# A four-layer decoder trunk: norms, output projections and router logits by token tiles

## The reference

```
for i in range(4):
    y = mixer[i % 3](h)                     # ends in a projection @ w_out to 1024 columns
    h = layer_norm(ALPHA * h + y, ln_mix_g[i], ln_mix_b[i])
    m = grouped_moe(h, w_router, ...)       # scores = sigmoid(h @ w_router); best group, top 2
    h = layer_norm(ALPHA * h + m, ln_ffn_g[i], ln_ffn_b[i])
```

## Time and profile before

| | us |
|---|---|
| Runs of the kernel | 2247.17 median of 3 (2244.17 to 2249.45) |
| The profiled execution | 2245.62, its span 2243.7 |
| TensorE matmul busy | 1977.2 (88% of the span) |
| VectorE busy | 760.4 (34%) |
| ScalarE busy | 492.8 (22%) |
| GpSimd busy | 158.8 (7%) |
| Mean granted TensorE clock | 0.928 of 2.4 GHz |
| Read from device memory | 501.80 MB, 224 GB/s over the span |

### The profile page before, as it was taken

One profiled execution on the slowest core, in us unless ns is written; L12 is line 12 of the kernel. 1 busy time (PEld: TensorE's weight loads), 2 busy tenths in 40 slices (PEclk: granted clock), 3 DMA queues, 4 the chain that ended last, 5 costly groups with the idle time before them and its releaser, 6 DMA issues.

```text
span 2243.7 us, 26143 instructions
## 1 busy us (share of the span) xinstructions
PE 1977.2 (88%) x9378; PEld 1137.2 (51%) x9379; DVE 760.4 (34%) x1564; ACT 492.8 (22%) x941; POOL 158.8 (7%) x96
## 2 busy tenths in 40 slices
PE   6989878999896768889989987899989989679997
PEld 5858744444573443443444534434468678334443
DVE  2435533332304343123322113233344265433324
ACT  2453311222203111012211101112223533111121
POOL 1010020000200030000020003000020000020000
PEclk8999988999996779889999997899989999879999
DMA  9430015999942139338994324679964400249994
GB/s 308 148 115 1 20 75 237 424 427 424 335 166 75 38 121 386 150 131 364 425 337 165 139 107 165 271 327 428 424 245 150 150 1 20 75 164 394 424 424 203
DMA packets 79872, 504.05 MB, mean 225 GB/s; under 512 B 7155, under 2 KB 11300, under 8 KB 54956
## 3 DMA queue, kind: packets, MB, share of 16 engines
q1 hardware_dynamic: 69536, 487.60, 53.9%
q0 software_dynamic: 2304, 8.39, 1.0%
q10 hardware_dynamic: 7948, 6.89, 1.0%
HBM read 501.80 MB, written 1.06 MB: 224 GB/s over the span
## 4 chain that ended last, share of the span: by engine, by line
PE 85%; DVE 10%; issue 3%; ACT 2%; ACTq 1%; DVEq 0%; DMA 0%
PE bank L1662 22%; PE bank L1680 11%; PE bank L1394 10%; PE bank L1400 9%; PE bank L1653 7%; PE bank L1778 5%; PE bank L1420 4%; PE bank L1627 2%; PE bank L1492 1%; PE bank L1483 1%; PE bank L1673 1%; PE bank L1385 1%; PE bank L1497 1%; PE bank L1726 1%; PE bank L1636 1%
## 5 line engine op out<-in xcount | busy, mean ns | idle before, releaser
L1662 PE MATMUL bank<-ring,work 128*64 128x512 f32 x2176 | 489.7, 609 | 15.5 <-DVE work L1231 9.5
L1662 PEld LDWEIGHTS bank<-ring,work 128*64 128x64 f32 x2176 | 156.7, 140 | 339.5 <-issue 332.6
L1680 PE MATMUL bank<-ring,work 128*64 128x512 f32 x1088 | 243.1, 596 | 8.6 <-ACT work L814 4.6
L1394 PE MATMUL bank<-HT,ring 128*128 128x256 f32 x1024 | 229.5, 384 | 0.9 <-DVE HT L865 0.9
L1394 PEld LDWEIGHTS bank<-HT,ring 128*128 128x128 f32 x1024 | 197.6, 193 | 37.3 <-issue 10.7
L1400 PE MATMUL bank<-ring,HT 128*128 128x512 f32 x448 | 195.0, 597 | 1.0 <-DVE HT L865 1.0
L1258 DVE TENSOR_TENSOR work<-bank,work 64x512 f32<-64x512 f32 x64 | 68.2, 1066 | 366.7 <-ACT work L792 366.7
L1653 PE MATMUL bank<-work 128*128 128x128 f32 x1152 | 157.1, 293 | 11.6 <-DVE work L1236 6.7
L1653 PEld LDWEIGHTS bank<-work 128*128 128x128 f32 x1152 | 143.4, 203 | 40.9 <-issue 31.6
L792 ACT ACTIVATE work<-bank 64x512 f32<-64x512 f32 x64 | 37.7, 589 | 526.7 <-PE bank L1662 526.7
L1226 DVE TENSOR_TENSOR work<-bank,lncols 128x512 f32<-128x512 f32 x72 | 49.8, 692 | 302.6 <-PE bank L1653 302.6
(11 more groups left out here) (284 smaller groups left out, 1996.5 us busy)
## 6 DMA issues: line engine op xcount, KB each, us to landing
ring<-in_e_w SPq DMA_DIRECT2D x192, 2048.0 KB, 13.2
ring<-in_a_w_in SPq DMA_DIRECT2D x16, 2048.0 KB, 14.9
ring<-in_c_w_in SPq DMA_DIRECT2D x8, 2048.0 KB, 14.5
ring<-in_b_w_in SPq DMA_DIRECT2D x6, 2048.0 KB, 17.1
ring<-in_a_w_out SPq DMA_DIRECT2D x4, 2048.0 KB, 7.8
ring<-in_c_w_out SPq DMA_DIRECT2D x4, 2048.0 KB, 7.8
ring<-in_b_w_out SPq DMA_DIRECT2D x2, 2048.0 KB, 9.3
gB<-in_ln_mix_g POOLq DMA_DIRECT2D x4, 512.0 KB, 4.1
```

The costliest lines, as they stand in the source:

```text
L1394: ins = mm(dst[:, 0:SEQ], wt[:, k, n * P:(n + 1) * P], HT[:, k, :], start=k == 0, stop=k == KC - 1)
L1662: ins = mm(bank[b][lo:lo + CAP, :], x[:, k, :], wt[:, k, :], start=k == 0, stop=k == KC - 1, skip_group_check=True)
L1680: ins = mm(bank[b][nh * CAP:(nh + 1) * CAP, :], h[:, m, :], w2[:, m, nh * 512:(nh + 1) * 512], start=m == 0, stop=m == 3, skip_group_check ...
```

## The change

- `plan()` gives phases one turn for each chunk and tile, tile 0's eight before tile 1's, on banks 0 to 3 (`k % 4`). `half` places a chunk with `k` below 4 in the lower 256 columns of the bank, the others in the upper. The router's turn goes to bank 4.
- The output projections run tile by tile: both halves of tile 0 and then of tile 1. All their weight units are awaited ahead of the first.
- The norm goes by tiles on VectorE: add, statistics, `rstd`, L908 and the four odd copies of tile 0, then the same for tile 1. ScalarE's root and copies go in the same order. At the experts' end and in the last phase it is the same, and in the gMLP's own norm `rstd` goes by tiles.
- TensorE at a mixer's end: transposes of tile 0, router logits of tile 0, then both for tile 1. At the experts' end: transposes of tile 0, then of tile 1, each behind its own `xhat_ready`.
- GpSimd's and ScalarE's waits on transposes go by the last tile's turn.

The core of the diff:

```diff
@@ -96,8 +96,12 @@
             unit(w_out[:, nh * 512:(nh + 1) * 512].rearrange("(k p) n -> p k n", p=P), ("y", i, TT - 1, nh))
-    for k in range(KC):
-        turns.take(k, "ht", 0, k)
+    def chunks(phase):
+        for tt in range(TT):
+            for k in range(KC):
+                turns.take(k % 4, "ht", phase, k, tt)
+
+    chunks(0)
     turns.take(0, "cols")
...
@@ -398,6 +400,10 @@
             eng.wait_ge(drained[b], n + 1)
+        def half(k, tt):
+
+            return slice(k // 4 * SEQ + tt * P, k // 4 * SEQ + (tt + 1) * P)
+
         def emptied(ins, *key):
...
@@ -584,15 +590,15 @@
             act.dma_start(rel33[0:REL_BUCKETS, :], w["rel_bias"]).then_inc(params_in, 16)
-            def ht_chunks(phase):
+            def ht_chunks(phase, tt):
                 for k in range(0, KC, 2):
-                    ps = wait_data(act, "ht", phase, k)
+                    ps = wait_data(act, "ht", phase, k, tt)[:, half(k, tt)]
+                    dst = HT[:, k, tt * P:(tt + 1) * P]
                     if phase == 0:
-                        emptied(a(HT[:, k, :], ps[:, 0:SEQ], ACT.Copy), "ht", phase, k)
+                        emptied(a(dst, ps, ACT.Copy), "ht", phase, k, tt)
                     else:
                         c = (0 if phase % 2 else 2) * 32 + (phase - 1) // 2 * 8 + k
-                        emptied(a(HT[:, k, :], ps[:, 0:SEQ], ACT.Identity, scale=lncols[:, c:c + 1],
-                                  bias=lncols[:, c + 32:c + 33]), "ht", phase, k)
+                        emptied(a(dst, ps, ACT.Identity, scale=lncols[:, c:c + 1], bias=lncols[:, c + 32:c + 33]), "ht", phase, k, tt)
             ln_count = 0
...
@@ -602,13 +608,14 @@
             rsq = 0
-            def ln_rstd():
+            def ln_rstd(tt):
                 nonlocal rsq
                 rsq += 1
-                ahead(ACT.Sqrt)
+                if not tt:
+                    ahead(ACT.Sqrt)
                 act.wait_ge(var_ready, rsq)
-                a(rs[:, 0, :], mv[:, :, 1], ACT.Sqrt, bias=epsc[:, 0:1]).then_inc(rstd_ready, 1)
+                a(rs[:, 0, tt:tt + 1], mv[:, tt, 1:2], ACT.Sqrt, bias=epsc[:, 0:1]).then_inc(rstd_ready, 1)
             def heads_norm(nn):
...
@@ -840,14 +849,17 @@
                     gmlp(i, j)
-                ln_rstd()
-                if 2 * i + 1 != last_phase:
-                    ht_chunks(2 * i + 1)
+                for tt in range(TT):
+                    ln_rstd(tt)
+                    if 2 * i + 1 != last_phase:
+                        ht_chunks(2 * i + 1, tt)
                 if with_moe:
                     experts(i)
-                    ln_rstd()
-                if i < n_layers - 1:
-                    ht_chunks(2 * i + 2)
+                for tt in range(TT):
+                    if with_moe:
+                        ln_rstd(tt)
+                    if i < n_layers - 1:
+                        ht_chunks(2 * i + 2, tt)
         @block.vector
...
@@ -855,69 +867,59 @@
-            def ht_chunks(phase):
+            def ht_chunks(phase, tt):
                 for k in range(1, KC, 2):
-                    ps = wait_data(dve, "ht", phase, k)
+                    ps = wait_data(dve, "ht", phase, k, tt)[:, half(k, tt)]
+                    dst = HT[:, k, tt * P:(tt + 1) * P]
                     if phase == 0:
-                        emptied(v.tensor_copy(HT[:, k, :], ps[:, 0:SEQ]), "ht", phase, k)
+                        emptied(v.tensor_copy(dst, ps), "ht", phase, k, tt)
                     else:
                         c = (0 if phase % 2 else 2) * 32 + (phase - 1) // 2 * 8 + k
-                        emptied(v.tensor_scalar(HT[:, k, :], ps[:, 0:SEQ], lncols[:, c:c + 1], lncols[:, c + 32:c + 33],
-                                                ALU.mult, ALU.add), "ht", phase, k)
+                        emptied(v.tensor_scalar(dst, ps, lncols[:, c:c + 1], lncols[:, c + 32:c + 33], ALU.mult, ALU.add), "ht", phase, k, tt)
...
-            def rstd(blocks):
+            def rstd(blocks, tt):
                 nonlocal rsq
                 own.wait()
-                for tt in range(TT):
-                    ins = v.bn_aggr(mv[:, tt, :], stats[:, tt, 0:6 * blocks])
-                    if tt < TT - 1:
-                        own.then(ins)
                 rsq += 1
-                ins.then_inc(var_ready, 1)
+                v.bn_aggr(mv[:, tt, :], stats[:, tt, 0:6 * blocks]).then_inc(var_ready, 1)
                 dve.wait_ge(rstd_ready, rsq)
-                own.link(v.reciprocal(rs[:, 0, :], rs[:, 0, :]))
...
+                r = [rs[:, n, tt:tt + 1] for n in range(4)]
+                own.link(v.reciprocal(r[0], r[0]))
...
+            def layer_norm(phase, tt):
+                rstd(2, tt)
...
-                for tt in range(TT):
-                    dst, src = H[:, tt, :], H[:, tt, :]
-                    if phase % 2:
-                        dst, src = XH[:, tt, :].rearrange("t (k p) -> t k p", k=KC), src.rearrange("t (p k) -> t k p", k=KC)
-                    v.tensor_scalar(dst, src, mv[:, tt, 0:1], rs[:, 3, tt:tt + 1],
-                                    ALU.subtract, ALU.mult).then_inc(xhat_ready, 1)
-
-            def add_mixed(i):
+                dst, src = H[:, tt, :], H[:, tt, :]
+                if phase % 2:
+                    dst, src = XH[:, tt, :].rearrange("t (k p) -> t k p", k=KC), src.rearrange("t (p k) -> t k p", k=KC)
+                v.tensor_scalar(dst, src, mv[:, tt, 0:1], rs[:, 3, tt:tt + 1], ALU.subtract, ALU.mult).then_inc(xhat_ready, 1)
+
+            def add_mixed(i, tt):
                 for nh in range(2):
-                    for tt in range(TT):
-                        ps = wait_data(dve, "y", i, tt, nh)
-                        sl = H[:, tt, nh * 512:(nh + 1) * 512]
-                        emptied(v.tensor_tensor(sl, ps[:, :], sl, ALU.add), "y", i, tt, nh)
-                    for tt in range(TT):
-                        wait_copy(dve, "y", i, tt, nh)
-                        block_stats(H, tt, nh)
+                    ps = wait_data(dve, "y", i, tt, nh)
+                    sl = H[:, tt, nh * 512:(nh + 1) * 512]
+                    emptied(v.tensor_tensor(sl, ps[:, :], sl, ALU.add), "y", i, tt, nh)
+                for nh in range(2):
+                    wait_copy(dve, "y", i, tt, nh)
+                    block_stats(H, tt, nh)
...
@@ -1300,9 +1302,13 @@
                         v.tensor_tensor(part(b), bank[b][:, :], part(b), ALU.add).then_inc(drained[b], 1)
-                for b in range(4, 8):
-                    dve.wait_ge(drained[b], first[b] + E // 2)
-                    block_stats(H, (b - 4) // 2, (b - 4) % 2)
+                for tt in range(TT):
+                    for nh in range(2):
+                        dve.wait_ge(drained[4 + 2 * tt + nh], first[4 + 2 * tt + nh] + E // 2)
+                        block_stats(H, tt, nh)
+                    layer_norm(2 * i + 2, tt)
+                    if i < n_layers - 1:
+                        ht_chunks(2 * i + 2, tt)
             steps_done = dve.alloc_register("steps_done_dve")
...
@@ -1377,16 +1380,16 @@
                 return ring[s]
-            def ht_chunks(phase):
+            def ht_chunks(phase, tt):
                 src = XH if phase % 2 else H
                 for k in range(KC):
-                    ps = fill("ht", phase, k)
-                    for tt in range(TT):
-                        ins = tr(ps[:, tt * P:(tt + 1) * P], src[:, tt, k * P:(k + 1) * P], ident)
-                    done(ins, "ht", phase, k)
-                if phase % 2 == 0:
+                    ps = fill("ht", phase, k, tt)
+                    done(tr(ps[:, half(k, tt)], src[:, tt, k * P:(k + 1) * P], ident), "ht", phase, k, tt)
+
+            def ht_in(phase):
+                for tt in range(TT):
                     for k in range(KC):
-                        wait_copy(pe, "ht", phase, k)
+                        wait_copy(pe, "ht", phase, k, tt)
             def rows(dst, wt, n):
...
@@ -1412,12 +1415,12 @@
                     wait_copy(pe, "oT", i, g)
-                for nh in range(2):
-                    wt = next_unit()
-                    for tt in range(TT):
+                wts = [next_unit(), next_unit()]
+                for tt in range(TT):
+                    for nh in range(2):
                         ps = fill("y", i, tt, nh)
                         for h in range(HEADS):
-                            ins = mm(ps[:, :], XT[:, h, tt * P:(tt + 1) * P], wt[:, h, :], start=h == 0, stop=h == HEADS - 1)
+                            ins = mm(ps[:, :], XT[:, h, tt * P:(tt + 1) * P], wts[nh][:, h, :], start=h == 0, stop=h == HEADS - 1)
                         done(ins, "y", i, tt, nh)
...
@@ -1619,20 +1622,23 @@
                     wait_copy(pe, "uT", i, g)
-                for nh in range(2):
-                    pss = [fill("y", i, tt, nh) for tt in range(TT)]
-                    wts = [next_unit(), next_unit()]
-                    for tt in range(TT):
```

(49 more changed lines are left out.)

54 lines of the change are left out of this document (21 added, 33 removed).

## The result

The changed kernel takes 2258.61 us (median of 8 runs, 2253.36 to 2260.77), the kernel before 2245.90 beside it (8 runs). The ratio is 1.0056, 95% interval 1.0042 to 1.0070: 12.7 us slower. Forecast were 20.3 slower, 2266, in a range from 2254 to 2275.

What follows compares the result with a forecast made beforehand. TensorE was 85% of the chain, so time could come only from its waits. Mixers 6.0, experts' ends 9.3, clock 1.0, output 1.6 and start 2.4 sum to 20.3 on 2245.6: forecast 2266 us, range 2254 to 2275.

Steps and rivals of the forecast that it cites:

- the experts' ends: Behind the experts, three places: 13.2 us instead of 10.1 to the next layer's first matmul; +9.3, bounds +2.4 and +4.2 each.
- the output: At the output: the norm chain of 1.6 us runs twice; +1.6, bounds +1.2 and +1.8.
- the start: At the start: with four banks, tile 0's transposes wait for ScalarE's first copy; +2.4, bounds +1.8 and +3.0.
- the clock at layer 1: Layer 1's first matmuls may begin at the low clock after two bursts of transposes; +1.0, for this end alone.
- The mixers' term: Behind four mixers: copies delay tile 1, GpSimd and gather (T+29.5; T: last projection's end); +6.0, bounds +3.2 and +9.6.
- gMLP, ring and residual at nothing: gMLP's norm by tiles, later-freed weights and output units awaited ahead, and GpSimd's residual 1.65 us later: all costed at nothing.
- Rival A: Behind the mixers: routing not tied to GpSimd's start, gather at T+27.5, -2.2 instead of +6.0; 2257.7 us; chance 0.14.
- Rival B: Behind the mixers: GpSimd holds none of the routing, gather at T+23.8, -17.0; 2243 or 2239 us; chance 0.06.

Runs made afterwards that it cites:

- the 2220 us kernel: Kernel before with only mixers by token tiles, GpSimd's residual begun after the first gather's shift, ScalarE alone copying tile 0 behind the mixers: 2220.03 us, ratio 0.9874.

## Why the prediction was right, and where its terms were off

The direction was right, and so was its main cause, the second chain of small steps at the experts' ends, the output and the start: these were forecast at 14.3 with the clock at layer 1, and cost 14 to 15 when made alone. The mixers' term had the right mechanism and the wrong result. It was forecast at +6.0, its gathers came 2.15 later, and taken alone the mixers' order made the kernel 5 to 6 us faster (2.3 against the changed code with everything put back). That the total still fell near the forecast rests on the other terms. The sizes, with the profile's 14.8 for the forecast's 20.3:

- **Mixers, +6.0 forecast, +2.15 measured** (by the gathers). The mechanism held: four copies ahead of tile 1's add, GpSimd later, the gather tied to it. Three sizes were off. VectorE is free at T+1.8, not 2.3, since the copies of the earlier trace rows at half width take 0.38 and bank releases 0.2. GpSimd starts at T+7.2 and not T+7.75. And the gather follows it by 21.4, not 21.8: from the end of the second addition it is 11.0 instead of 11.4. The bound of +3.2 was still too high. (The prediction's own 0.5+4x0.41 is 2.1 and not 2.0; its 2.3 stands between the bounds all the same.)
- **Experts' ends, +9.3 forecast, +7.9 measured.** 12.9 for 13.2, since the transposes with their bank waits took 2.1 us and not 2.3 (0.8 in all); and the forecast took before's 10.1 from layer 0 for all three, while layers 1 and 2 had 10.44 and 10.29 (0.5). The bounds of +2.4 and +4.2 do not come out of the terms named: without the two bank waits and with copies of 0.27 it is +2.2, with 0.5 for each wait and 0.54 for the copy +3.8.
- **The clock at layer 1's start, +1.0 forecast, +2.9 between these two profiles** (that layer's first 80 matmuls 20.43 against 17.50 us), and 0.5 at each of the two later starts. This was the term with the worst reading: I let the clock be low for 3 us of matmuls, and it was low for 5.9, and through both bursts of transposes before them. By the rule that the Trainium skill gives (TensorE: Matmul & The Clock Gate, "Part 1: The HAM clock gate") only sustained activity releases the high clock; the trace agrees, 0.50 until 611. But most of the 2.9 is the state in which before was caught. With both tiles together at the experts' end these 80 matmuls took 17.50 in three profiles and 19.4 to 19.9 in eight; with the ends by tiles 20.43, 19.82 and 20.20, some 0.5 more than the eight. Layer 2's start goes the other way: 36.2 in before and one more profile, 34.6 in nine, 36.4 to 36.7 with the ends by tiles. The rest of layer 1's 4.6 is the clock as well: in after it was low until 768.3, over the first 3.2 us of the output projection, which costs 1.5; in before it had risen just ahead of it.
- **Output +1.6 forecast, +1.6 measured. Start +2.4 forecast, +2.0 measured** at the first parameter transpose: the wait for ScalarE and the three rounds of four, all there.
- **gMLP, ring and residual at nothing:** the mixers of layers 2 and 3 are 0.6 and 0.7 longer, which is the clock term of 0.5.
- **What no step named: -4.4.** The experts begin at the high clock in more layers of this profile (1 and 3, which give 3.9 of it). The prediction read the clock only at the experts' ends, and behind the mixers it had the earlier trace rows in hand: the first gather takes 5.80 in layer 0 and 6.73 in layer 2, the same 32 matmuls.

Rival A (routing not tied to GpSimd) lands at 2257.7, nearest to the measured time, and is wrong all the same: L1155 ends with GpSimd's addition, and without GpSimd the routing's held step takes 0.19. It comes that near by luck. Its gathers would be 2.2 earlier and are 2.15 later; the 4.4 that no step named cover that error. Rival B's gain was there to be had, but only by moving GpSimd: 5.3 us a layer.

## What to carry to other kernels

A split by tiles pays where the first tile's norm lies under work, and costs its second chain of small steps where nothing covers it; split only there. When the step behind the split waits for another engine (here GpSimd's start), an earlier input gains nothing until that engine is moved: find the hold, then split. And where TensorE's work comes in short bursts, read the granted clock in them and in the work behind them: two matmuls of 0.5 us in an idle gap, in each layer, were worth 12 us here. What a higher clock is worth in the work behind them is an estimate from profiles, and the one test of it did not confirm it.

## What the runs showed of the hardware

- VectorE's product of two small tiles beside GpSimd's additions of two tiles took 1.89 to 2.24 us, to the end of GpSimd's instruction, and 0.19 with GpSimd away. The reciprocal just ahead of it took its 0.35 with GpSimd running. Beside GpSimd's scaling (one tile and a constant) some of these products took 0.89 to 1.01 us, and most their 0.16.
- Sixteen matmuls of 16 columns took 1.86 us at the high and 3.43 at the low clock, and the clock fell between tile 0's and tile 1's, at 787.2 in layer 1 of the 2220 us kernel, while TensorE was transposing. Two added matmuls, 1.1 us together, held it in three layers of four.
- In the first pass over the experts TensorE stood up to 3.2 us (2.6 in layer 0) for what looks like its own instructions, behind gathers at 0.81 as well as at 1.00. A granted clock of 0.91 instead of 0.80 in the first 22 us goes with some 2.2 us less in layers 0 and 3. At 1.00 layer 0's experts took 246.2 and 246.7, 2 us more than at 0.91 without added matmuls; layer 2's took 276.3, against 277.0 to 279.6 at 0.90 to 0.93.
